# The input projection of a hybrid mLSTM layer as Strassen block products

## The reference

```
parts_x = _split_proj((_rmsnorm(x, norm_w) * (1 + scale) + shift) @ in_w)
parts_c = _split_proj((_rmsnorm(xc, norm_w) * (1 + scale_c) + shift_c) @ in_w)
...
y_m = _mlstm_branch(h_x, parts_x, head_norm_w, branch_m_w)
y_p = _pool_branch(parts_x, (rows, GRID_W), (1, 2), pool_w, pool_scale, branch_p_w)
x = x + gate * _merge(parts_x, y_m, y_p, out_w)
```

## Time and profile before

| | us |
|---|---|
| runs (3): median | 2493.97 |
| lowest, highest | 2491.96, 2496.21 |
| the profiled execution | 2491.28 |
| its span, first to last instruction | 2489.4 |

### The profile page before, as it was taken

One profiled execution on the slowest core, in us unless ns is written; L12 is line 12 of the kernel. 1 busy time (PEld: TensorE's weight loads), 2 busy tenths in 40 slices (PEclk: granted clock), 3 DMA queues, 4 the chain that ended last, 5 costly groups with the idle time before them and its releaser, 6 DMA issues. The chain is left out here.

```text
span 2489.4 us, 35553 instructions
## 1 busy us (share of the span) xinstructions
PE 2378.3 (96%) x12835; PEld 2025.7 (81%) x12835; DVE 1201.5 (48%) x2317; ACT 820.4 (33%) x1694; POOL 334.5 (13%) x336
## 2 busy tenths in 40 slices
PE   7889999999999999999999999999999689999998
PEld 5668888888888877888888888888888578797978
DVE  3512212222222224666666756676666355656564
ACT  3521111111111112343444434444443434343532
POOL 0120000000000002122213211222120112121210
PEclk9999999999999999999999999999999799999999
DMA  9347666656756636766676696766766555656663
GB/s 289 94 76 264 132 118 168 139 124 152 168 110 153 161 85 224 234 233 220 198 235 223 217 333 231 240 219 201 232 218 224 173 161 191 207 193 202 198 203 111
DMA packets 443094, 470.23 MB, mean 189 GB/s; under 512 B 24320, under 2 KB 359820, under 8 KB 437420
## 3 DMA queue, kind: packets, MB, share of 16 engines
q1 hardware_dynamic: 428124, 395.60, 52.5%
q0 software_dynamic: 9280, 38.79, 6.9%
q10 hardware_dynamic: 5520, 33.56, 3.8%
HBM read 327.66 MB, written 156.98 MB: 195 GB/s over the span
## 5 line engine op out<-in xcount | busy, mean ns | idle before, releaser
L1270 PE MATMUL bank<-xlate,wh 128*128 128x512 f32 x2048 | 670.9, 401 | 8.0 <-DVE v_t L1404 4.7
L1270 PEld LDWEIGHTS bank<-xlate,wh 128*128 128x128 f32 x2048 | 373.6, 189 | 77.4 <-DVE v_t L1404 5.1
L1270 PE MATMUL bank<-xlate,wl 128*128 128x512 f32 x1024 | 410.0, 400 | 0.0
L697 PE MATMUL bank<-xearly,wh 128*128 128x512 f32 (+1 forms) x1280 | 367.3, 372 | 0.0
L697 PE MATMUL bank<-xlate,wh 128*128 128x512 f32 x1024 | 321.7, 395 | 0.0
L697 PEld LDWEIGHTS bank<-xearly,wh 128*128 128x128 f32 x1280 | 228.4, 188 | 39.0
L697 PE MATMUL bank<-xearly,wl 128*128 128x512 f32 (+1 forms) x640 | 236.6, 370 | 0.0
L697 PEld LDWEIGHTS bank<-xlate,wh 128*128 128x128 f32 x1024 | 190.8, 189 | 39.1
L1270 PEld LDWEIGHTS bank<-xlate,wl 128*128 128x128 f32 x1024 | 193.7, 189 | 34.1
L697 PE MATMUL bank<-xlate,wl 128*128 128x512 f32 x512 | 201.2, 393 | 0.0
L907 DVE SCALAR_TENSOR_TENSOR qks<-bank,qks 128x512 fp32r<-128x512 f32 (+1 forms) x72 | 47.5, 660 | 284.2 <-ACT qks L773 284.2
(11 more groups left out here) (272 smaller groups left out, 4595.8 us busy)
## 6 DMA issues: line engine op xcount, KB each, us to landing
v_t<-vk_d SPq DMA_DIRECT2D x144, 384.0 KB, 3.7
qk_d<-qks SPq DMA_DIRECT2D x64, 512.0 KB, 3.4
q_t<-qk_d SPq DMA_DIRECT2D x128, 256.0 KB, 4.2
wraw<-wpair_d ACTq DMA_DIRECT2D x31, 1024.0 KB, 6.7
wraw<-in_in_w_dram SPq DMA_DIRECT2D x32, 512.0 KB, 9.9
vk_d<-vs SPq DMA_DIRECT2D x64, 256.0 KB, 4.0
wpair_d<-in_in_w_dram POOLq DMA_DIRECT2D x16, 1024.0 KB, 13.7
k_t<-qk_d SPq DMA_DIRECT2D x64, 256.0 KB, 5.3
```

What stands on the lines that cost most here:

```text
L697: mm = pe.matmul(bank[m % 4][:, 0:w], a[:, u % 2, k, :], xn(b, k, t0, w), start=(k == 0 and n == 0), stop=(k == KT - 1 and n == 2))
L1270: mm = pe.matmul(bank[m % 2][:, :], a[:, u % 2, k, :], xlate[part][:, k, tq * TQ:(tq + 1) * TQ], start=(k == 0 and n == 0), stop=(k == KT ...
```

## The change

The projection of the latent tokens is now computed half by half (1024 tokens each), and in each half by Strassen's scheme in the form with seven products. A unit is one pair of 128-column tiles (256 columns: the q, k or v of a head, or p beside z_p; kind "s"), times 1024 tokens in two quarters, with the 1024 channels in two halves. Its 2x2 block product had eight block products of 4 channel tiles; now there are seven, M1 to M7, 12 matmuls each (L1106). 32 units make 232 positions (POS), with eight E positions for the context, whose other products are issued between the matmuls of M1, M2 and M4 (L1110).

Token side: the operands are four blocks B and four combinations T1 to T4, computed once per half. The early half is combined and split in the opening, by DVE, ACT and POOL. The late half is combined there too, stored unsplit (xr_d, 32 blocks of 256 KB) and loaded back and split, block by block, while unit 15 (UA) and unit 16 run (RB, RB_AT: 28 blocks at positions 112 to 123, two or three each; four more at the end). The context comes last in the opening instead of first.

Weight side: POOL makes the four sums of each unit (ssum, L974 to L989), ACT and DVE split an operand of 512 elements for each product, three positions ahead; wh and wl are rings of four operands. Weights are loaded once for each half, 1 MB a unit.

Result side: DVE adds products out of PSUM with u2 (M1+M6 and so on) into tmp, ACT and POOL (or DVE) split q and k from there.

The gate columns of the late quarters are computed at positions 134 and 135, and the chain of small steps is spread over the positions after them. The work of two heads was a loop; now everything is written out. Low parts of q and k move from DVE to POOL. Cut to its core:

```diff
-        xlate = [late.enter_context(nc.sbuf_tensor(f"xlate{n}", [P, KT, HALF], FP32R, side="right")) for n in range(2)]
-        xearly = [early.enter_context(nc.sbuf_tensor(f"xearly{n}", [P, KT, CTX + HALF], FP32R, side="right")) for n in range(2)]
+        xlate = [late.enter_context(nc.sbuf_tensor(f"xlate{n}", [P, 4, KH, TQ], FP32R, side="right")) for n in range(2)]
+        xtop = [early.enter_context(nc.sbuf_tensor(f"xtop{n}", [P, 3, KH, TQ], FP32R, side="right")) for n in range(2)]
+        xctx = [early.enter_context(nc.sbuf_tensor(f"xctx{n}", [P, KT, CTX], FP32R, side="right")) for n in range(2)]
...
+        xr_d = scratch("xr_d", (8, KH, P, TQ))
...
+        XPIECES = [(half, s // 2, kd + KH * (s % 2)) for half in range(2) for kd in range(KH) for s in range(4)]
+        XPIECES += [(None, 0, j) for j in range(KT)]
...
+                def part_12(kd):
+                    sp.wait_ge(b_hi_act, 3 * kd + 3)
+                    sp.wait_ge(b_lo, 4 * kd + 3)
+                    for part in range(2):
+                        sp.dma_start(xe_d[part, :, kd, TQ:2 * TQ], f32(xtop[part][:, 2, kd])).then_inc(b12_stored[kd], 16)
...
+                for kd in range(KH):
+                    for s in range(4):
+                        sp.wait_ge(y_made, NPH + 4 * kd + s + 1)
+                        sp.dma_start(xr_d[B_RAW[s], kd], slot(kd, s)).then_inc(y_stored[kd % 2], 16)
+                    sp.wait_ge(late_pool, kd + 1)
+                    sp.wait_ge(late_dve, 3 * kd + 3)
+                    for n in range(4):
+                        sp.dma_start(xr_d[T_RAW[n], kd], tsum[:, 4 * (kd % 3) + n]).then_inc(t_stored[kd % 3], 16)
...
+                def low(kd, s, hi, lo):
+                    if s == 3:
+                        pool.wait_ge(b_hi_dve, kd + 1)
+                    else:
+                        pool.wait_ge(b_hi_act, 3 * kd + s + 1)
+                    pool.tensor_tensor(lo, slot(kd, s), f32(hi), ALU.subtract).then_inc(b_lo, 1)
...
+                def high_low(n, kd, dst, s, low=True):
+                    dve.tensor_copy(dst[0], slot(kd, s)).then_inc(t_hi, 1)
+                    if low:
+                        dve.wait_ge(t_hi, 4 * kd + n + 1)
+                        dve.tensor_tensor(dst[1], slot(kd, s), f32(dst[0]), ALU.subtract).then_inc(t_lo_dve, 1)
...
+                    dve.wait_ge(b_hi_act, 3 * kd + 1)
+                    dve.wait_ge(b_lo, 4 * kd + 1)
+                    dve.tensor_tensor(slot(kd, 0), slot(kd, 2), slot(kd, 0), ALU.subtract).then_inc(t_add, 1)
+                    dve.wait_ge(t_add, 4 * kd + 1)
+                    high_low(0, kd, T1, 0)
+                    if kd < 2:
...
+                    dve.tensor_tensor(slot(kd, 2), slot(kd, 3), slot(kd, 2), ALU.subtract).then_inc(t_add, 1)
+                    dve.wait_ge(t_add, 4 * kd + 2)
+                    high_low(1, kd, T3, 2)
...
+                    dve.wait_ge(b_lo, 4 * kd + 4)
+                    dve.tensor_tensor(slot(kd, 3), slot(kd, 3), slot(kd, 0), ALU.subtract).then_inc(t_add, 1)
+                    dve.wait_ge(t_add, 4 * kd + 3)
+                    dve.tensor_tensor(slot(kd, 1), slot(kd, 1), slot(kd, 3), ALU.subtract).then_inc(t_add, 1)
...
+                    dve.wait_ge(t_add, 4 * kd + 4)
+                    dve.wait_ge(b12_stored[kd], 32)
+                    high_low(3, kd, T4, 1, low=False)
...
+                    dve.wait_ge(y_made, NPH + 4 * kd + 4)
+                    if kd >= 3:
+                        dve.wait_ge(t_stored[kd % 3], 64)
+                    g = 4 * (kd % 3)
+                    dve.tensor_tensor(tsum[:, g], slot(kd, 2), slot(kd, 0), ALU.subtract).then_inc(late_dve, 1)
+                    dve.wait_ge(late_dve, 3 * kd + 1)
+                    dve.tensor_tensor(tsum[:, g + 2], slot(kd, 3), tsum[:, g], ALU.subtract).then_inc(late_dve, 1)
+                    dve.wait_ge(late_dve, 3 * kd + 2)
+                    dve.tensor_tensor(tsum[:, g + 3], slot(kd, 1), tsum[:, g + 2], ALU.subtract).then_inc(late_dve, 1)
...
-            UNITS = [(t, kind) for t in range(HB) for kind in "qkv"] + [(0, "p"), (0, "s")]
...
-            PIECES = [(u, t, kind, t0, w) for u, (t, kind) in enumerate(UNITS)
-                      for t0, w in ([cpiece] if kind in "kv" else []) + xpieces]
...
+            UNITS = [(0, i, kind) for i in range(HEADS - 1) for kind in "qvsk"] + [(0, HEADS - 1, kind) for kind in "vkqs"]
+            UNITS += [(1, i, kind) for kinds in ("qs", "vk") for i in range(HEADS) for kind in kinds]
...
+            POS = []
+            for u in range(NU + 1):
+                if u < NU:
+                    POS.append((u, "M1"))
+                if u:
+                    POS += [(u - 1, n) for n in ("M4", "E", "M3") if n != "E" or with_context(u - 1)]
+                if u < NU:
+                    POS += [(u, n) for n in ("M2", "M6", "M5", "M7")]
...
+            MADE = {"M2": "C11", "M7": "C22", "M4": "C21", "E": "CX", "M3": "C12"}
...
+            RB = [("M1", 0, R_B11), ("M2", 1, R_B21), ("M6", 4, R_T2), ("M5", 3, R_T1), ("M7", 5, R_T3), ("M4", 6, R_T4),
+                  ("M3", 2, R_B22)]
+            UA = NU // 2 - 1
+            RB_AT, at = [], AT[UA, "M1"] + 1
+            for n, b, raw in RB:
+                for kd in range(KH):
+                    at = max(at, AT[UA, n] + 1)
+                    while RB_AT.count(at) >= (2 if at < AT[UA, "M5"] else 3):
+                        at += 1
+                    RB_AT.append(at)
...
+            PBANK = {"M1": bank[0], "M2": bank[1], "M6": bank[2], "M5": bank[3], "M7": bank[1], "M4": bank[3], "M3": bank[2]}
...
+                def block_in(n):
+                    if n >= NST:
+                        b = n - NST
+                        sp.wait_ge(rb_lo_pool if rb_on_pool(b) else rb_lo_dve, RB_POOL[b + 1] if rb_on_pool(b) else b + 1 - RB_POOL[b + 1])
+                    raw = RB[n // KH][2]
+                    sp.dma_start(stage[:, n % NST], xr_d[raw, n % KH]).then_inc(st_loaded[n % NST], 16)
...
+                    for (kh, tq), b in BLOCK_OF.items():
+                        if b < 3:
+                            pool.dma_start(xe_d[part, :, KH * kh:KH * (kh + 1), tq * TQ:(tq + 1) * TQ], f32(xlate[part][:, b])).then_inc(xe_stored, 16)
...
+                def sums(u, n):
+                    raw_need = 32 * (u // 2 + 1)
+                    pool.wait_ge(raw_loaded[u % 2], raw_need)
+                    if n == 1:
+                        if u:
+                            pool.wait_ge(op_lo, AT[u - 1, "M5"] + 1)
+                        pool.tensor_tensor(ssum[:, 0], raw_block(u, 0, 1), raw_block(u, 1, 1), ALU.add).then_inc(s_made, 1)
+                    elif n == 2:
+                        if u:
+                            pool.wait_ge(op_lo, AT[u - 1, "M6"] + 1)
+                        pool.wait_ge(s_made, 4 * u + 1)
+                        pool.tensor_tensor(ssum[:, 1], ssum[:, 0], raw_block(u, 0, 0), ALU.subtract).then_inc(s_made, 1)
+                    elif n == 3:
+                        if u:
+                            pool.wait_ge(op_lo, AT[u - 1, "M7"] + 1)
+                        pool.tensor_tensor(ssum[:, 2], raw_block(u, 0, 0), raw_block(u, 0, 1), ALU.subtract).then_inc(s_made, 1)
+                    else:
+                        pool.wait_ge(op_lo, AT[u, "M2"] + 1)
+                        pool.wait_ge(s_made, 4 * u + 2)
+                        pool.tensor_tensor(raw_block(u, 1, 0), raw_block(u, 1, 0), ssum[:, 1], ALU.subtract).then_inc(s_made, 1)
...
+                def low(a):
+                    part = os[:, nos[a] % NOS]
+                    pool.wait_ge(qk_hi, nqk[a] + 1)
+                    pool.tensor_tensor(part[:, :, 1, :], tmp[:, a % NTM].rearrange("p (c t) -> p c t", t=P),
+                                       f32(part[:, :, 0, :]), ALU.subtract).then_inc(qk_lo, 1)
...
+                def product(p):
+                    u, name = POS[p]
+                    half = UNITS[u][0]
+                    pe.wait_ge(op_hi, p + 1)
+                    pe.wait_ge(op_lo, p + 1)
...
+                    elif name == "M6" and u:
+                        pe.wait_ge(c12_made, u)
+                    elif name == "M5" and u:
+                        pe.wait_ge(c21_made, u)
...
+                        pe.wait_ge(u2_made, u + 1)
+                    if half == 1 and u == UA + 1:
+                        rebuilt(name)
...
+                    if ctx_of and ctx_of[2] and ctx_of[0] == 0 and nctx[u] >= 2:
+                        pe.wait_ge(cx_made, nctx[u] - 1)
+                    for kd in range(KH):
+                        for n, (a, part) in enumerate(((w_hi_, 0), (w_hi_, 1), (w_lo_, 0))):
+                            if dst is not None:
...
+                for p in range(NSTEPS):
...
+                    for n in range(2):
+                        if p == G0 + n:
+                            gates(CB[n], TQ, quarter_terms(n))
...
+                def split_hi(p):
```

(42 more changed lines are left out.)

1151 lines of the change are left out of this document (697 added, 454 removed).

## The result

The changed kernel takes 2521.15 us (median of 4 runs, 2520.28 to 2526.68) where the kernel before took 2492.97 in the same comparison: the ratio is 1.0116, with a 95% interval of 1.0098 to 1.0133. It is slower by 28 us; the forecast was 2449, 44 us faster, and its range ended at 2490. The profiled execution is the slowest of the four (2526.68); its span is 2524.8 us, 35.4 more than the earlier trace rows.

What follows compares the result with a forecast made beforehand. PE was taken to set the projection's pace. Terms -87.8 - 15 + 9.1 - 2 + 34 + 5 + 10 + 2 = -44.7 us brought the span from 2489.4 to 2444.7, forecast 2449 us; likeliest case 2433 to 2465, range 2420 to 2490.

Steps and rivals of the forecast that it cites:

- Step (6): Projection units: the other engines and weight loads can feed PE, at +5 us in all, bounds 0 and +20.
- step (2): Gate chain spread over 28 and more positions: 11 us of wait and about 4 of slow matmuls go, -15 us.
- step (7): Change of half, positions 112 to 123: rebuilding 28 blocks costs +10 us, bounds 0 and +25.
- Steps (1) and (3): Projection matmuls at 0.2287 us: 384 fewer, -87.8 us; the last quarter's gate columns need three blocks, +9.1 us.
- Step (4): From the opening's end to the first product: 22 us in place of 23.9, -2 us.
- Step (5): Opening: later weights, rounds with DVE and POOL one after the other, late-half stores; 142 us against 108.2, +34, bounds +21 and +50.
- first rival: Everything fits: DVE and POOL overlap in the opening (-13), no stalls at the change of half or elsewhere: 2421 us, chance 0.18.
- Step (8): End of the projection: the last unit is k, its add, splits and store take 6.4 us for 4, +2 us.
- The second: Rival: DMA and shared work cost more, change of half +25, opening +45 or unit stalls 16: about 2480 us, chance 0.15.
- The third: Rival: M6 waits in each unit because DVE stands behind POOL; up to +102, 2550 us, chance 0.11.
- The fourth: Rival: gain and opening cancel, with opening +50, stalls 25, change of half 20: about 2492 us, chance 0.04.
- ACT waiting on weights: One of the signs listed as showing the forecast wrong, beside PE waiting in every unit; no size given.

Runs made afterwards that it cites:

- e15: Kernel before the change, without the 16 copies of the scan block's weights, which are read from the input: 2509.6 us, ratio 1.0062.
- e1: Changed kernel without GpSimd's 16 copies of the scan block's weights; the scan block reads them from the input: 2492.5 us, ratio 0.9988.
- e11: Changed kernel without the copies, and with two neighbouring column tiles of one kind for units of p and z: 2476.9 us, ratio 0.9923.
- e14: e11 with the late half's rebuilding cut to 32 of 512 columns, so arithmetic is left out: 2460.8 us, ratio 0.9872.
- e4: Changed kernel with the late half's rebuilding cut to 32 of 512 columns in loads, copies and subtractions: 2513.6 us, ratio 1.0074.
- e10: Changed kernel with the weight sums moved from GpSimd to VectorE, everything computed: 2508.4 us, ratio 1.0049.
- e2: Changed kernel with all 16 copies kept but issued four positions after a unit's M1, none in units 14 to 17: 2517.9 us, ratio 1.0094.
- e5: Changed kernel whose eight units of p and z take two neighbouring column tiles of one kind, in rows of 1024 bytes: 2510.2 us, ratio 1.0054.
- e6: Changed kernel with unit 17's weights issued in eight pieces of 128 KB, one behind each of the rebuild's loads: 2523.5 us, ratio 1.0108.
- e8: Changed kernel with GpSimd's 20 low parts of the opening cut to 4 of 512 columns: 2513.7 us, ratio 1.0068.
- e9: Changed kernel with the opening's 20 low parts moved from GpSimd to VectorE, nothing left out: 2522.1 us, ratio 1.0106.

## Why the prediction was wrong

**Step (6) failed**, and within it these sentences: "Weights: 1 MB a unit lands in 9.6 us, issued six positions (16 us) before need" and "Bursts may queue, on the whole it fits". The lead was about right: a unit's first product starts 15.6 us after the issue or later, and waits begin behind pairs that land 14 to 16 us after it (1.1 us behind 14.4, 2.6 behind 16.0; unit 10's 19.1 met none). The landing was not a constant. It went from 8.4 to 25.2 us with what else stood in the queues. The forecast's 9.6 us is one single load at the end; in the kernel before, loads of half that size took from 5.7 to 27.5 us, the longest while the early half was stored, and the row gives only their median, 10.0. The copies, which take 0.14 of the engines' time, are in the 114 MB, but in no term of the sum. The mean share was close (0.75 measured, some 0.8 forecast), but a mean says nothing of a stretch of 12 us in which one queue has 96%. Before the change all 16 copies cost about 1 us (e15).

How much is it? Matmuls less and more, and the old stall gone, make 803.9 - 87.8 + 9.1 - 14.4 = 710.8 us, and 798.8 was measured: 88 us over, of which 3 stand at the end. Counted as the time from start to start of PE's matmuls over 0.2287, 0.118 and 0.088 us, less the 10 us of it that the kernel before has outside its two waits, it is 31 us around the change (520 to 600 us) and 53 elsewhere; 67 of these 84 are the waits, the rest is the slow clock behind them. Some 8 of the 53 stand at the gate chain's new place and belong to step (2). So step (6) was +45 for +5, outside its bounds of 0 and +20, step (7) +31 for +10, outside 0 and +25, and step (2) -7 for -15. These 69 us are nearly all of the 80 by which the spans differ (2524.8 for 2444.7). e1 gives 44 of them back by the copies alone and e11 64.

**Step (7)** named VectorE and GpSimd one after the other and the rebuild's bandwidth, 350 GB/s asked of 335. Both are there (e14), but 335 comes from stores of the early half. Weights from the input moved 89 GB/s at a share of 1.00 in e1 (762 to 770 us). Megabytes of different kinds were added as if they cost the engines the same, and spread over 33 us as if none of them had to land first; the rebuild's loads stood behind a copy and a unit's weights. In its own terms, +10 was +31.

**Steps (1) and (3)** held: the matmuls keep their 0.2287 us. **Step (2)** held in part: the gate chain's 11 us wait is gone, but one of 5.7 us stands at its new place, where the forecast had none. There VectorE's first step of the chain stands beside GpSimd's work:

```profile
670.23 4.85 DVE L1276 TENSOR_TENSOR gparts<-gparts 72x128 f32<-72x128 f32 x1 [0.58 <-DMA gparts<-gates_d]
675.01 0.28 DVE L1277 TENSOR_TENSOR gparts<-gparts 72x128 f32<-72x128 f32 x1
```

```profile
671.05 1.37 POOL L994 TENSOR_TENSOR os<-tmp,os 128x512 fp32r<-128x512 f32 x1
672.31 1.37 POOL L984 TENSOR_TENSOR ssum<-wraw 128x512 f32<-128x512 f32 x1
673.55 1.37 POOL L994 TENSOR_TENSOR os<-tmp,os 128x512 fp32r<-128x512 f32 x1
```

An operation of 0.28 us took 4.85, and ended 0.16 us after the last of GpSimd's in a row. The same operation took 0.28 and 0.29 us in e4 and e10, where GpSimd did nothing beside it, 1.38 to 1.40 in eight runs in which it ended with or shortly behind one operation of GpSimd, 3.00 in e2 behind two, and 4.90 to 5.31 in e5, e6, e8 and e9 behind four. By the Trainium skill, "SBUF — State Buffer", section "Who interferes with whom", the port that the two share is an exclusive lock; the trace agrees, and shows that back-to-back operations of GpSimd need not let VectorE in between. It is not the only cause of the wait: in e10 the operation was short and the wait at this place 8.8 us. There VectorE had idled 10.2 us for the chain's own load (`gparts<-gates_d`), and ACT 11.3 us for VectorE, with PE's next splits in order behind them. In e11 the wait is 1.1 us.

**Step (4)**: 22.5 us for 22. **Step (5)**: +39 for +34, inside its bounds: the rounds ended at 111.7 (forecast 112), the late half took 28.5 us for 24 to the context, which took 7 for 6. The working stands: e8 shows GpSimd's lows on the path, 12.5 us where the first rival's term had 13. **Step (8)**: the last wait is 7.8 us where it was 4.7, +3 for +2.

**The rivals.** The second had the mechanism, "DMA and the shared work cost more", with a price of +25 and +16 where 31 and 45 came, so that it ended below the kernel before. The third, a wait of M6 in each unit, did not come: 14 waits in 32 units, most of their time behind late weights and blocks. The time fell among the slower outcomes, which had a chance of 0.11, but not by the mechanism that they had. (The fourth's terms add up to 2495 and not 2492, still within 0.2%.) The text named "ACT waiting on weights" as what would be wrong, and that is what happened; it gave it no price.

**What stays open.** Why GpSimd's copy had nearly all of the engines at 791 us but 48% at 564 and 49% in the kernel before (520 to 534 us). A packet of it took 0.87 us in the mean at 791, from the fence above, and 0.37 at 564, so it was slow itself there. The Trainium skill, "DMA: Bandwidth & Descriptors", section "Queues, rings and completion order", says that an engine takes turns between queues, a packet at a time; a share of 48 beside 49 for SP's queue fits it, 96 beside 0.6 doesn't, and no run here tells why. Why the rest of the program is 8 to 16 us longer without the copies was not taken apart beyond the load's 13.0 for 6.5 us. Nor is it known what the 24 us are made of that e11's projection still lies above the 710.8, but for the 13.4 us wait and the slow clock behind it.

## What to carry to other kernels

When a change makes a stretch shorter, list every transfer in it, those of later stages too, and lay the largest ones against the slack of a single load: what was hidden with 22 us of matmuls a load may stand on the path when a load of twice the size comes every 19. Price a transfer by its own kind of rows, not by a bandwidth of another kind, and ask of a burst and of the longest landing, not of a mean or a median. When waits carry many names, follow the timeline to the first instruction that started late; here a late transfer stood behind most of them.
